# Down products of a pass's last expert bank by bank, with additions and statistics waiting for each bank

## What is computed

```python
def hier_moe(x, wg, bg, we, be, w_gate_up, w_down):
    # 4 groups of 4 experts; a token goes to one group and to two of its experts
    hu = jnp.einsum('td,edf->tef', xt, w_gate_up)
    hg, hv = jnp.split(hu, 2, axis=-1)
    act = jax.nn.silu(hg) * hv * gates[..., None].astype(x.dtype)
    out = jnp.einsum('tef,efd->td', act, w_down)
    ...
        ffn = hier_moe(x, moe_router_g_w[i], moe_router_g_b[i], moe_router_e_w[i], moe_router_e_b[i],
                       moe_w_gate_up[i], moe_w_down[i])
        x = layer_norm(DEEPNORM_ALPHA * x + ffn, ln_g[i, 1], ln_b[i, 1])
```

## Time and profile before

| | us |
|---|---|
| median of three runs | 1527.9 (1526.47 to 1528.75) |
| the profiled execution | 1528.34 |
| its span from first to last instruction | 1526.6 |
| TensorE busy | 1414.1 |
| DVE busy | 486.0 |
| ScalarE busy | 371.5 |
| mean granted TensorE clock | 0.974 |

### The profile page before, as it was taken

How to read it: one execution, slowest core, us unless ns; L and a number is a source line. 1 busy time by engine, 2 the same in 40 slices (tenths; PEclk the granted TensorE clock), 3 DMA queues, 4 the chain that set the end, 5 groups by cost and what they waited for, 6 DMA issues and landing times.

```text
span 1526.6 us, 20558 instructions
## 1 busy us (share of the span) xinstructions
PE 1414.1 (93%) x9004; PEld 779.3 (51%) x9004; DVE 486.0 (32%) x1021; ACT 371.5 (24%) x559; POOL 21.7 (1%) x33
## 2 busy tenths in 40 slices
PE   6999999999799999998898998879999999889894
PEld 6999998998553333332243346454333333224331
DVE  5867767544431020020002027633003003002202
ACT  4566556432401021021012021230102102101100
POOL 0000000000000000000000000000000000000000
PEclk9999999999999999999999999989999999999998
DMA  9855544744279999999999984348999999999992
GB/s 300 267 156 164 165 151 137 243 160 166 92 309 421 427 408 428 427 427 427 428 427 426 430 343 189 122 131 347 427 428 402 429 427 428 427 427 428 424 428 107
DMA packets 91622, 492.23 MB, mean 322 GB/s; under 512 B 5357, under 2 KB 61613, under 8 KB 63693
## 3 DMA queue, kind: packets, MB, share of 16 engines
q1 hardware_dynamic: 84320, 466.11, 76.0%
q0 software_dynamic: 2672, 15.21, 2.5%
q10 hardware_dynamic: 4538, 9.59, 2.0%
HBM read 478.77 MB, written 16.04 MB: 324 GB/s over the span
## 4 chain that ended last, share of the span: by engine, by line
PE 72%; DMA 18%; DVE 6%; issue 2%; ACT 1%; DVEq 0%; POOL 0%; SPq 0%; ACTq 0%; POOLq 0%
PE ps L1062 20%; PE ps L1079 19%; DMA ring<-in_moe_w_down 16%; PE ps L991 5%; PE ps L884 5%; PE ps L885 4%; PE ps L886 4%; PE ps L937 2%; PE ps L938 2%; PE ps L939 2%; PE ps L898 2%; PE ps L1140 2%; PE ps L1016 2%; DMA ring<-in_lru_w_in 1%; DMA xtok<-x_rows,src_now 1%
## 5 line engine op out<-in xcount | busy, mean ns | idle before, releaser
L1062 PE MATMUL ps<-ring,xsel 128*64 128x512 f32 x2048 | 465.4, 606 | 20.3 <-DMA ring<-in_moe_w_gate_up 20.3
L1079 PE MATMUL ps<-ring,work 128*32 128x512 f32 x3072 | 346.2, 595 | 12.6 <-DMA ring<-in_moe_w_down 12.6
L1062 PEld LDWEIGHTS ps<-ring,xsel 128*64 128x64 f32 x2048 | 142.3, 139 | 314.8 <-issue 275.3
L1079 PEld LDWEIGHTS ps<-ring,work 128*32 128x32 f32 x3072 | 91.7, 109 | 224.1 <-issue 204.1
L1611 DVE SCALAR_TENSOR_TENSOR arena<-arena,ps 64x512 f32<-64x512 f32 x32 | 21.7, 679 | 551.5 <-ACT work L768 551.5
L884 PE MATMUL ps<-operands,whi 128*128 128x288 f32 x512 | 153.4, 300 | 1.5 <-DVE ring_lo L1219 1.5
L885 PE MATMUL ps<-ring_lo,whi 128*128 128x288 f32 x512 | 151.6, 296 | 0.0
L886 PE MATMUL ps<-operands,ring_lo 128*128 128x288 f32 x512 | 150.7, 294 | 0.0
L1219 DVE TENSOR_TENSOR ring_lo<-ring,whi 128x1024 fp32r<-128x1024 f32 x96 | 115.7, 1223 | 76.6 <-ACT whi L591 76.4
L591 ACT ACTIVATE whi<-ring 128x1024 fp32r<-128x1024 f32 x96 | 100.7, 1057 | 140.7 <-PE ps L886 85.4
L767 ACT ACTIVATE arena<-ps 64x512 f32<-64x512 f32 x32 | 18.9, 590 | 394.7 <-PE ps L1062 394.6
(11 more groups left out here) (308 smaller groups left out, 1165.1 us busy)
## 6 DMA issues: line engine op xcount, KB each, us to landing
ring<-in_moe_w_gate_up SPq DMA_DIRECT2D x128, 2048.0 KB, 19.2
ring<-in_moe_w_down SPq DMA_DIRECT2D x64, 2048.0 KB, 19.4
ring<-in_lru_w_in SPq DMA_DIRECT2D x16, 2048.0 KB, 9.9
ring<-in_lru_w_out SPq DMA_DIRECT2D x8, 2048.0 KB, 12.1
x_rows<-xtok ACTq DMA_DIRECT2D x4, 1024.0 KB, 3.9
ring<-in_pool_w SPq DMA_DIRECT2D x4, 1024.0 KB, 13.0
xtok<-in_x_prompt SPq DMA_DIRECT2D x2, 1024.0 KB, 9.5
ring<-in_lru_w_a SPq DMA_DIRECT2D x8, 256.0 KB, 5.7
```

The source lines that it names most:

```text
L1062: last = mm(ps[half * ES:(half + 1) * ES, e % 2, :], xsel[:, k, e * ES:(e + 1) * ES], wt[:, half * 512:(half + 1) * 512], start=(k == 0), ...
L1079: last = mm(ps[rows:rows + QB, 2 + r, :], act[:, e % 2, f * W + slots0:f * W + slots0 + QB], wt[:, d * 512:(d + 1) * 512], start=start, st ...
```

## The change

Only the last expert of a pass (`e == NE - 1`) gets another order of its rounds: bank outside, f inside, so that bank 0 takes f = 0 to 3, then bank 1, then bank 2. The number of rounds in each of its eight parts stays 2, 1, 2, 1 and so on; `LAST_ROUNDS` lists them, and the weights are taken from block 22 or 23 by f. Since the first bank needs both blocks, TensorE waits for block 23 too before the first part. Bank 0 is complete after part 3 of 8, bank 1 after part 5, bank 2 after part 8; `BANK_DONE` says so as counts before the end, and DVE waits for each bank by itself (before: once for banks 0 and 1 after part 7, once for bank 2). Since block 22 is now read until the last part, the block that follows in its slot (`last == -2`) waits for the end of the pass.

```diff
+LAST_ROUNDS = [(r, f) for r in range(3) for f in range(KF)]
+BANK_DONE = (-5, -3, 0)
...
-                            eng.wait_ge(parts_used, snap(seq * PARTS_WIN + parts_before(l, last + 1)))
+                            eng.wait_ge(parts_used, snap(seq * PARTS_WIN + parts_before(l, last + (2 if last == -2 else 1))))
...
-                            f = q // 2
+                            if e == NE - 1 and q == 0:
+                                eng.wait_ge(ring_ready[slot_of(n + 1)], seq * 64 + ready_at(n + 1))
...
-                            wt = ring_at(n)[:, (f % 2) * D:(f % 2 + 1) * D]
-                            start, stop = e == 0 and f == 0, e == NE - 1 and f == KF - 1
-                            for r in ((0, 1), (2,))[q % 2]:
+                            if e == NE - 1:
+                                rounds = LAST_ROUNDS[q // 2 * 3 + q % 2 * 2:q // 2 * 3 + q % 2 + 2]
+                            else:
+                                rounds = [(r, q // 2) for r in ((0, 1), (2,))[q % 2]]
+                            for r, f in rounds:
+                                wt = ring_at(n - q // PARTS_CHUNK + f // 2)[:, (f % 2) * D:(f % 2 + 1) * D]
+                                start, stop = e == 0 and f == 0, e == NE - 1 and f == KF - 1
...
-                            if b % 2 == 0:
-                                eng.wait_ge(parts_used, seq * PARTS_WIN + (parts_base(l) + NPART + (-1 if b == 0 else 0)))
+                            if b < 3:
+                                eng.wait_ge(parts_used, seq * PARTS_WIN + (parts_base(l) + NPART + BANK_DONE[b]))
...
-                    if b % 2 == 0:
-                        eng.wait_ge(parts_used, eng.snap((n_win + extra) * PARTS_WIN + (parts_base(l) + NPART - (b == 0))))
+                    if b < 3:
+                        eng.wait_ge(parts_used, eng.snap((n_win + extra) * PARTS_WIN + (parts_base(l) + NPART + BANK_DONE[b])))
```

## The result

The change makes the kernel slower. The changed kernel took 1548.7 us (median of 4 runs, 1545.1 to 1552.6) against 1528.3 for the kernel before; the ratio on record is 1.0118, with a 95% interval of 1.0097 to 1.0139, or +18.0 us (+14.8 to +21.2). It is not the quotient of the two medians, which differ by 20.3 us (1.0133). In the experiments too the times in us behind a ratio are worked out from the ratio. Forecast were 1543.0, +15.1, and a range of 1537 to 1549. One execution of the kernel before, beside e0 to e3, took 1951.3 us at a granted clock of 0.689 and is left out of the ratios. The profiled execution of the changed kernel took 1552.6 us, with a span of 1550.8, and is the slowest of the four.

The account below looks back on a forecast made before the run. The prediction took the DMA queue as the bound from pass 1 on. Per layer 4.1 + 1.6 + 3.0 - 1.2 = +7.5 us, two layers +15.0, span 1541.6, plus 1.7, less 0.4: 1543.0 us; range 1537 to 1549.

Parts of the forecast that it names:

- the shift between pass 0 and 1: Block 4 issued only at pass 0's end, queue run dry: later blocks shift 4.1 us per layer (3.4 to 4.9).
- block 5's surplus: Pass 1, layer 1: block 5 landed 7.0 us after block 4, not 4.9; if that stays, the shift is 4.9.
- the one row from an idle queue: Profile row where a block issued into an idle queue landed after 7.8 us; the latency the forecast kept.
- the estimate of 6.8: Skill page's figure in us for a block from an idle queue; by it the sum would be 1541.
- The shift between pass 1 and 2: Block 4 of pass 2, issued at pass 1's end, adds 1.6 us per layer (0 to 1.8), total 5.7.
- pass 2 to 3: Block 4's issue moves 8 us but still finds three blocks in front of it: cost 0.
- the wait for block 23: Before the last expert, TensorE waits for this landing: 3.0 us per layer in pass 3, free in pass 2.
- the tail: At each layer's end, early additions of banks 0 and 1 gain 1.24 us (0 to 1.3).
- rival A: The clock falls after the new waits: 2.9 us once per layer in the last pass, 1548.9 us; chance 14%.
- a granted clock of 0.5 in the last expert: Sign named beforehand as showing the forecast wrong: the clock at half speed during the last expert.
- B: The late block is absorbed by slack in passes 1 to 3: +3.5 us, 1531.4 us; chance 8%.
- C: Not slower: the queue drains its backlog faster, 2.7% per block, and makes the gap up: 1525.4 us; chance 6%.

Follow-up runs that it names:

- e0: The changed kernel run again with no edit: 1548.4 us, ratio 1.0103 to the kernel before.
- e3: The changed kernel with DVE waiting for banks 0 and 1 as before the change, nearly at the products' end: 1549.3 us, ratio 1.0128.
- e1: The kernel before with only the later SP wait, block 4 waiting for the end of the pass before: 1547.0 us, ratio 1.0101.
- e2: The kernel before with only the added TensorE wait for block 23 ahead of the last expert: 1536.6 us, ratio 1.0047.
- e4: The changed kernel with the change kept in pass 3 alone, passes 0 to 2 in the old order: 1536.7 us, ratio 1.0038.

## Why the prediction came out as it did

**Right: the bound and the direction.** The queue of transfers bounds passes 1 to 3, and what it loses while dry stays to the end of the layer. e1 isolates it: +5.9 and +6.5 us, where parts (a pass 0 to 1, a pass 1 to 2) said 5.7.

**Mis-sized: the shift between pass 0 and 1.** I took 4.1 as the middle of 3.4 and 4.9. Against TensorE's own shift, the blocks of the second half of pass 1 land 4.5 to 4.8 us later in four profiles with the late slot, so nearly the whole moved block. The low end supposed that block 5's surplus would vanish; it came back in the blocks behind. Against the one row from an idle queue, 7.8 us, block 4 took 8.0 us (7.9 to 8.0) in layer 0 and 8.9 to 9.1 in layer 1; the estimate of 6.8 that stands beside that row was too low for these transfers, which SP issues. The shift between pass 1 and 2 measured 1.5 to 1.8 (forecast 1.6). At pass 2 to 3 nothing was lost, as forecast.

**Right: the wait for block 23**, paid once a layer: 3.7 and 3.3 us in e2 (forecast 3.0), and absorbed in pass 2. **Right: the tail**, 1.27 us (forecast 1.24) and 1.2 by e3's tail.

**In part: rival A.** I gave the falling clock 14% and 2.9 us in each layer. It fell after the wait of pass 3 in layer 1, where the 96 instructions took 11.82 us instead of 10.51, so 1.3 us; in layer 0, whose wait was 1.83 us, it did not. In e0 it was the same (11.85 and 10.51 us), in e3 it fell in neither. After pass 2's waits it fell too and cost 1.7 and 1.5 us (12.20 and 12.03), which pass 3 absorbed. So the mechanism was real, half as dear and paid in one layer. The prediction named a granted clock of 0.5 in the last expert as a sign against its forecast, which had put this term at nothing; the clock was 0.50 from 1520.9 to 1523.4, in the last expert of layer 1, and so on this point the forecast was wrong.

**The sum again, by measured terms.** Layer 0: 5.9 (e1) + 3.7 (e2) = 9.6; measured 9.3. Layer 1: 6.5 + 3.3 + 1.3 for the clock = 11.1; measured 12.2. Less 2.5 for the two tails: 18.2, where the profiles give 9.3 + 12.2 - 2.5 = 19.0 and the runs 18.0 (14.8 to 21.2). The forecast's terms, 15.0 (1543.3 less 0.4 is 1542.9, not 1543.0), lacked 1.0 us for the shift, 1.3 for the clock and 1.0 for the waits, and had 0.1 too little for the tails. The last 1.1 us in layer 1 is a later landing of block 23 in pass 3, seen in e0, e1, e3 and e4 as well; its cause stays open.

**Rivals B and C** are refuted: the stretch of e1 grew by the whole dry time, and the blocks behind the gap landed 4.9 us apart or more, but for single pairs of 4.7 that follow a longer one.

**Not foreseen:** that the beginning of the kernel differs by up to 8 us between executions, which I had no view of from a single profile.

**Overlooked in the change.** Its description says that block 22 is read until the last part. By `LAST_ROUNDS` its last round (bank 2, f = 1) lies in part 7 of 8, so the wait for the end of the pass is one round longer than the products need, an estimated 0.9 us (8 of the 96 instructions that take 10.51). No run tried the earlier release.

## What to carry to other kernels

The ring of deep transfers here hid a late consumer but not a late release: before work is regrouped across two blocks, ask which block comes free later and whether the queue still has something to move by then. What a reordering is to gain in a tail often needs only a part of it: here completing the banks within the second block gave the same 1.3 us a layer and kept both blocks' times. Effects of 1 to 3 us in a kernel that varies by 10 us are read by distances within a profile, with the runs only as bounds.

## What the runs showed of the hardware

The granted clock after a wait of about 3 us is not settled by the wait's length. It fell after waits of 2.86, 2.98 and 3.04 us in the changed kernel and 2.76 us in e0. In e2 it stayed at full speed (96 instructions in 10.51 us) after 2.96 and 3.02 us and fell after another wait of 2.96 us (12.20). After 1.83 and 2.05 us it stayed; after 4.46 us it was 0.50 for the next 5.33 us. What decides it is not shown. The Trainium skill, "TensorE: Matmul & The Clock Gate", section "HAM oscillation", describes waits for transfers after which every tile starts cold; by the waits of e2 that does not happen every time.

A 2 MB block issued into an empty or nearly empty queue (block 4 of passes 1 and 2 in the four profiles with the late slot) took 7.6 to 9.1 us to land, of which 4.9 are its time at 427 GB/s.
